# Feed-forward feature products: one instruction of 512 columns for both activation parts

## The reference, cut to what matters

```
def swiglu(x, w1, w3, w2):          # block 2, twice a layer
    return (silu(x @ w1) * (x @ w3)) @ w2
x = x + square(relu(h2 @ w_up)) @ w_down   # block 1, once a layer
```

## Time and profile before

| | us |
|---|---|
| median of 3 runs | 2420.14 (2417.0 to 2423.95) |
| the profiled execution | 2415.4 |
| its span | 2413.3 |
| TensorE busy | 2316.9 |
| VectorE busy | 1387.3 |
| ScalarE busy | 1118.4 |

### The profile page before, as it was taken

The page is one execution under the profiler, slowest core; times in us unless marked ns, Lnnn a source line. Parts: engine busy times, 40 slices in busy tenths (PEclk is TensorE's granted clock), DMA queues, the critical chain, the costliest instruction groups (busy, mean ns, idle before and its releaser), DMA issues.

```text
span 2413.3 us, 38462 instructions
## 1 busy us (share of the span) xinstructions
PE 2316.9 (96%) x16098; PEld 2123.8 (88%) x16098; DVE 1387.3 (57%) x1838; ACT 1118.4 (46%) x1737; POOL 186.8 (8%) x191
## 2 busy tenths in 40 slices
PE   7989999999999999999999999999999999998998
PEld 6988987887998998799998889979978999896997
DVE  5556555646654544655566764565565555776454
ACT  4754543573453444445443544444444444344442
POOL 0001210001120210000002001011100000110110
PEclk9999999999999999999999999999999999999999
DMA  6424555432555655564533545555555444263554
GB/s 215 136 97 148 181 198 172 167 123 100 180 187 188 220 184 189 163 181 140 168 109 119 174 164 182 187 201 184 187 167 184 154 157 141 79 205 125 187 180 141
DMA packets 109006, 395.93 MB, mean 164 GB/s; under 512 B 12375, under 2 KB 12545, under 8 KB 108577
## 3 DMA queue, kind: packets, MB, share of 16 engines
q1 hardware_dynamic: 104400, 377.53, 47.4%
q0 software_dynamic: 4432, 15.93, 2.0%
HBM read 392.92 MB, written 1.05 MB: 163 GB/s over the span
## 4 chain that ended last, share of the span: by engine, by line
PE 86%; DVE 7%; ACT 4%; DMA 2%; issue 1%; SPq 0%; DVEq 0%; ACTq 0%
PE psum L389 77%; DVE w_low L346 2%; PE psum L791 2%; PE psum L757 2%; DMA ring<-in_weights 2%; PE psum L693 2%; ACT w_high L343 1%; PE psum L775 1%; ACT attn_p L873 1%; DVE stats L563 1%; PE psum L1747 1%; DVE mx L817 0%; DVE xs L2059 0%; DVE xs L586 0%; DVE xT_low L652 0%
## 5 line engine op out<-in xcount | busy, mean ns | idle before, releaser
L346 DVE TENSOR_TENSOR w_low<-ring,w_high 128x1024 fp32r<-128x1024 f32 x704 | 863.0, 1255 | 588.3 <-ACT w_high L343 587.0
L343 ACT ACTIVATE w_high<-ring 128x1024 fp32r<-128x1024 f32 x704 | 717.5, 1053 | 295.0 <-DMA ring<-in_weights 294.9
L389 PE MATMUL psum<-xT_high,w_high 128*128 128x256 f32 x2976 | 848.7, 285 | 0.0
L389 PE MATMUL psum<-xT_low,w_high 128*128 128x256 f32 x2976 | 844.4, 284 | 0.0
L389 PE MATMUL psum<-xT_high,w_low 128*128 128x256 f32 x2976 | 844.3, 284 | 0.0
L389 PEld LDWEIGHTS psum<-xT_high,w_high 128*128 128x128 f32 x2976 | 573.0, 193 | 0.8
L389 PEld LDWEIGHTS psum<-xT_low,w_high 128*128 128x128 f32 x2976 | 573.1, 193 | 0.4
L389 PEld LDWEIGHTS psum<-xT_high,w_low 128*128 128x128 f32 x2976 | 573.0, 193 | 0.0
L389 PE MATMUL psum<-w_high,hidden 128*128 128x512 f32 x1216 | 377.0, 390 | 0.0
L389 PEld LDWEIGHTS psum<-w_high,hidden 128*128 128x128 f32 x1216 | 228.4, 188 | 47.0
L389 PE MATMUL psum<-w_low,hidden 128*128 128x512 f32 x608 | 236.8, 389 | 0.0
(11 more groups left out here) (233 smaller groups left out, 2201.9 us busy)
## 6 DMA issues: line engine op xcount, KB each, us to landing
ring<-in_weights SPq DMA_DIRECT2D x706, 512.0 KB, 3.6
pages<-in_affine POOLq DMA_DIRECT2D x16, 512.0 KB, 5.0
ring<-in_weights SPq DMA_DIRECT2D x8, 440.0 KB, 3.4
pages<-in_gains POOLq DMA_DIRECT2D x4, 512.0 KB, 5.1
pages<-in_mem POOLq DMA_DIRECT2D x2, 1024.0 KB, 6.2
ring<-in_weights SPq DMA_DIRECT2D x4, 384.0 KB, 3.2
x<-in_x_in SPq DMA_DIRECT2D x2, 512.0 KB, 4.5
pages<-in_rows POOLq DMA_DIRECT2D x2, 512.0 KB, 6.0
```

The source lines that it names most:

```text
L343: eng.activation(high, raw, ACT.Copy).then_inc(self.flag("w_rounded").sem, 1)
L346: eng.tensor_tensor(self.w_low[:, piece % SLOTS, 0:width], raw, high.bitcast(F32), ALU.subtract).then_inc(self.flag("w_split").sem, 1)
L389: m = pe.matmul(out, a, b, start=(first and i == 0), stop=(last and i == len(pairs) - 1))
```

## The change: what it does

`xT_high` and `xT_low` become the halves of one tensor `xT`. A new function `gemm_beside` gives each tile a bank of its own: per k a matmul of 256 columns (low weights by the high activation) into the bank's first half, and one of 512 columns (high weights by both activation parts, a moving operand of two runs of 256) into the whole bank. The first half then holds two of the three products and the second half the third. VectorE adds the halves with a `tensor_reduce` of 512 elements to 256 (`halves_added`). Block 1 takes 28 banks a layer for `up` in place of 14, block 2 takes 40 in a feed-forward part in place of 20. `gemm_features` stays for all other products.

In block 1 the maximum with zero moves from ScalarE to VectorE, in one instruction with the square. In block 2 silu reads the sum from SBUF. In both, the engines split weights after each tile, one piece a time.

```
-        self.xT_high = sb("xT_high", [P, KD, SEQ], F32R)
-        self.xT_low = sb("xT_low", [P, KD, SEQ], F32R)
+        self.xT = sb("xT", [P, 2, KD, SEQ], F32R)
+        self.xT_high, self.xT_low = self.xT[:, 0, :, :], self.xT[:, 1, :, :]
...
+    def gemm_beside(self, pe, l, stream, banks, group, act, kn, tile):
+        self.take_bank(pe, l, banks, group)
+        out = self.bank(banks, group)
+        for k in range(kn):
+            high, low = self.weight(pe, l, stream, (tile[0], tile[1], k))
+            act(k)
+            pe.matmul(out[:, 0:SEQ], low, self.xT_high[:, k, :], start=(k == 0), stop=False, skip_group_check=True)
+            m = pe.matmul(out.rearrange("p (x s) -> p x s", x=2), high, self.xT[:, :, k, :], start=False,
+                          stop=(k == kn - 1), skip_group_check=True)
+            if k == kn - 1:
+                m.then_inc(*self.flag("filled").one())
+            self.used(l, stream, (tile[0], tile[1], k), m, self.flag("filled").last(l) if k == kn - 1 else None)
+        self.piece_after[group] = self.piece_now
+
+    def halves_added(self, dve, l, banks, key, out):
+        h = self.filled(dve, l, banks, key)
+        dve.tensor_reduce(out, h.rearrange("p (x s) -> p s x", x=2), AX, ALU.add).then_inc(*self.drained(banks, key))
...
-                c.gemm_features(pe, l, stream, banks, "up", ("up", n), xTf, KD,
-                                [("up", 2 * n - 4), ("up", 2 * n - 3)])
+                for i in (2 * n, 2 * n + 1):
+                    c.gemm_beside(pe, l, stream, banks, ("up", i), xTf, KD, ("up", i - 4))
...
-                h = c.filled(act, l, banks, ("up", n))
-                act.wait_ge(*(c.flag("hidden_whole").at(l, n - 3) if n >= 4 else c.flag("first_whole").at(l, n - 1)))
-                act.activation(c.attn_p[:, n % 2, :], h, ACT.Relu).then_inc(*c.drained(banks, ("up", n)))
-                if n > 2:
-                    round_hidden(n - 1)
-                after(("up", n))
+                for i in (2 * n, 2 * n + 1):
+                    split(c.piece_after["up", i] + AHEAD)
+                    if i == 2 * n and n > 2:
+                        round_hidden(n - 1)
...
-                c.wait_drained(dve, l, banks, ("up", n))
-                if n >= 4:
-                    dve.wait_ge(*c.flag("hidden").at(l, n - 3))
-                dve.tensor_tensor(c.attn_pT[:, n % 2, :], c.attn_p[:, n % 2, :], c.attn_p[:, n % 2, :],
-                                  ALU.mult).then_inc(*c.flag("hidden_whole").one())
-                after(("up", n))
+                dve.wait_ge(*(c.flag("hidden").at(l, n - 3) if n >= 4 else c.flag("first_whole").at(l, n - 1)))
+                for i in (2 * n, 2 * n + 1):
+                    cut = slice(i % 2 * SEQ, (i % 2 + 1) * SEQ)
+                    c.halves_added(dve, l, banks, ("up", i), c.attn_p[:, n % 2, cut])
+                    c.wait_drained(dve, l, banks, ("up", i))
+                    sum_, whole = c.attn_p[:, n % 2, cut], c.attn_pT[:, n % 2, cut]
+                    dve.scalar_tensor_tensor(whole, sum_, 0.0, sum_, ALU.max, ALU.mult
+                                             ).then_inc(*c.flag("hidden_whole" if i % 2 else "dve_step").one())
+                    split(c.piece_after["up", i] + AHEAD)
...
-                    c.gemm_features(pe, l, stream, banks, f, (f, n), xT, KD, [(f + "a", n), (f + "b", n)])
+                    for x in "ab":
+                        c.gemm_beside(pe, l, stream, banks, (f + x, n), xT, KD, (f + x, n))
...
-                    if n >= 4:
-                        c.wait_drained(act, l, banks, (f + "t", n - 4) if n < 6 else (f, n - 4))
-                    act.activation(silu[:, n % 4, :], h[:, 0:SEQ], ACT.Silu).then_inc(*c.flag("silu").one())
...
+                    after_a = c.piece_after[f + "a", n] + AHEAD
+                    c.wait_drained(act, l, banks, (f + "a", n))
+                    act.activation(silu[:, n % 4, :], silu[:, n % 4, :], ACT.Silu).then_inc(*c.flag("silu").one())
                     if n > 2:
                         round_hidden(f, n - 1)
-                    after((f, n))
+                    split(after_a)
+                    after((f + "b", n))
...
-                    dve.tensor_tensor(gated[:, n % 4, :], silu[:, n % 4, :], c.bank(banks, key)[:, SEQ:2 * SEQ],
-                                      ALU.mult).then_inc(*c.drained(banks, key))
-                    after((f, n))
+                    elif n >= 4:
+                        c.wait_drained(dve, l, banks, (f + "t", n - 4))
+                    c.halves_added(dve, l, banks, (f + "a", n), silu[:, n % 4, :])
+                    after((f + "a", n))
+                    c.halves_added(dve, l, banks, (f + "b", n), gated[:, n % 4, :])
+                    dve.wait_ge(*c.flag("silu").at(l, done + n + 1))
+                    c.wait_drained(dve, l, banks, (f + "b", n))
+                    dve.tensor_tensor(gated[:, n % 4, :], silu[:, n % 4, :], gated[:, n % 4, :], ALU.mult
+                                      ).then_inc(*c.flag("gated").one())
+                    after((f + "b", n))
```

More of the change, by code:

```diff
@@ L990, in block_1 @@
             banks.add((key, n))
-    for key, n in (("out", 0), ("up", 16), ("down", 0)):
+    for key, n in (("out", 0), ("up", 32), ("down", 0)):
         for i in range(n):
-            banks.add(("upt", i) if i < 2 else (key, i))
+            if i not in (2, 3):
+                banks.add(("upt", i) if i < 2 else (key, i))
         if not n:
@@ L1520, in ffn_groups @@
         for n in range(KF2):
-            banks.add((f + "t", n) if n < 2 else (f, n))
+            if n < 2:
+                banks.add((f + "t", n))
+            else:
+                banks.add((f + "a", n))
+                banks.add((f + "b", n))
     def model_groups(key):
@@ L1831, in round_hidden @@
             def round_hidden(f, n):
-                c.wait_drained(act, l, banks, (f, n))
+                act.wait_ge(*c.flag("gated").at(l, (KF2 - 2 if f == "f2" else 0) + n - 1))
                 act.activation(c.hidden[KF2][0][:, n, :], gated[:, n % 4, :], ACT.Copy
@@ L1844, in ffn @@
                         beside()
-                    key = (f + "t", n) if n < 2 else (f, n)
-                    h = c.filled(act, l, banks, key)
-                    if n >= 4:
-                        c.wait_drained(act, l, banks, (f + "t", n - 4) if n < 6 else (f, n - 4))
-                    act.activation(silu[:, n % 4, :], h[:, 0:SEQ], ACT.Silu).then_inc(*c.flag("silu").one())
                     if n < 2:
+                        act.activation(silu[:, n % 4, :], c.filled(act, l, banks, (f + "t", n))[:, 0:SEQ], ACT.Silu
+                                       ).then_inc(*c.flag("silu").one())
                         if n == 1:
@@ L2038, in ffn @@
                         bias_low()
-                    dve.wait_ge(*c.flag("silu").at(l, done + n + 1))
-                    key = (f + "t", n) if n < 2 else (f, n)
+                    key = (f + "t", n)
                     if n < 2:
+                        dve.wait_ge(*c.flag("silu").at(l, done + n + 1))
                         dve.tensor_tensor(first[:, n, :], silu[:, n % 4, :], c.bank(banks, key)[:, SEQ:2 * SEQ], ALU.mult
@@ L2469 @@
                         "sb_valued", "osb_ready", "merged", "hidden_whole", "sink_less", "sink_exp"],
-           2: COMMON + ["params", "mem_loaded", "affine_in", "bias_cleared", "bias_rounded", "bias_parted", "pool_step", "silu", "bias_halved", "merged", "gmlp_normed",
+           2: COMMON + ["params", "mem_loaded", "affine_in", "bias_cleared", "bias_rounded", "bias_parted", "pool_step", "silu", "gated", "bias_halved", "merged", "gmlp_normed",
                         "spatial_ready", "spatially_mixed", "gmlp_gated", "convolved", "lat_ready", "n_roped",
@@ L2474 @@
 COUNTS = {
-    1: {'filled': 50,
-         'drained0': 13,
-         'drained1': 13,
-         'drained2': 12,
-         'drained3': 12,
-         'dve_step': 64,
+    1: {'filled': 64,
+         'drained0': 16,
+         'drained1': 16,
+         'drained2': 16,
+         'drained3': 16,
+         'dve_step': 78,
          'act_step': 16,
@@ L2512 @@
          'first_whole': 2},
-    2: {'filled': 123,
-         'drained0': 31,
-         'drained1': 31,
-         'drained2': 31,
-         'drained3': 30,
+    2: {'filled': 163,
+         'drained0': 41,
+         'drained1': 41,
+         'drained2': 41,
+         'drained3': 40,
          'dve_step': 165,
@@ L2555 @@
          'cmp_roped': 1,
-         'branch_gated': 2},
+         'branch_gated': 2,
+         'gated': 40},
 }
```

1 line of the change is left out of this document (added).

## The result

The changed kernel takes 2428.95 us (median of 8 runs, 2424.52 to 2433.23) against 2419.29 us for the kernel before in the same session (8 runs, 2415.73 to 2423.95): ratio 1.0039, 95% interval 1.0029 to 1.005. It is slower, by 9.7 us; the forecast was 2413.4 us. The value lies on the other side of no change. It is inside the range given (2398 to 2475) only because that range was drawn out to the dear reduce, which did not come true; the forecast's own range, 2403 to 2422, does not hold it.

The account below looks back on a forecast made before the run. TensorE was taken to bound the changed stages. From the profiled 2415.4 us, block 1 takes 6.0 and block 2 takes 0.7 (gain 17.1 against waits 16.4), giving 2408.7, or 2413.4 us on the median's scale; range 2398 to 2475.

Parts of the forecast that it names:

- the dear reduce: Rival: VectorE's reduce alternates between bank halves and takes 1.07 us, making block 2's loop 6.49 us; 2474 us, slower, chance 22%.
- the loop's sum of 5.73 us: Block 2: one VectorE and ScalarE round for two tiles takes 5.73 us against TensorE's 5.55, so VectorE falls behind 0.18 us.
- 0.02 (the product waits for it): Block 2's loop: the wait between the second reduce and VectorE's product, taken as 0.02 us on top of the reduce's 0.69.
- The pace of 0.3467 us a pair: TensorE, changed products: one 256-column and one 512-column matmul take 0.120 + 0.2267 = 0.3467 us, in place of 0.360.
- the gross gain: TensorE time saved by shorter products, before any waits: 23.0 us, of which 6.0 in block 1 and 17.1 in block 2.
- the third rival: The operand's second run costs another 13.3 ns, so a pair stays at 0.360 us; 2424.5 us, no change, chance 13%.
- -6.0 forecast: Block 1: VectorE needs 2.2 to 2.37 us a tile, under TensorE's 2.77, so the whole 6.0 us gain stays.
- L - 2.6 at the fourth bank: Block 2, start of each down product: TensorE waits VectorE's lateness L less 2.6 us; 2.2, 2.2, 4.2, 7.8, together 16.4 us.
- The limit beyond which products stop inside the stage: Block 2's feed-forward parts: VectorE's lateness over 7 us stalls products earlier, which costs the same microseconds.
- The cheap reduce: Rival: VectorE's reduce takes 0.42 us, block 2's loop is 5.19 us and hardly binds; 2398 us, faster, chance 10%.
- the forecast's own case: The main forecast without the rivals, chance 55%: range 2403 to 2422 us, split 0.23 faster, 0.30 within, 0.02 slower.
- three signs of being wrong: VectorE keeps level with TensorE in block 2, the reduce is away from 0.69 us by over 0.04, or block 1 shows waits.

Follow-up runs that it names:

- e1: Changed kernel, but in block 2 ScalarE rounds the weights five pieces ahead before waiting for the first reduce, not behind silu: 2399.85 us, ratio 0.9917 to the kernel before.
- e11: Changed kernel with VectorE's wait for silu moved ahead of the second reduce in block 2's loop: 2422.48 us, ratio 1.0017 to the kernel before.
- e4: Changed kernel with block 2 as in the kernel before, so only block 1 has the new form: 2415.39 us, ratio 0.9987 [0.9977, 0.9997].
- e9: Changed kernel with block 1 as in the kernel before, so only block 2 has the new form: 2435.14 us, ratio 1.0058 to the kernel before.
- e8: Changed kernel with one more VectorE instruction, a memset of 128 unused columns, in block 2's loop: 2434.8 us, ratio 1.0059 to the kernel before.

## Why the prediction failed

**The reason was right, one term of its sum was too small.** I said that VectorE falls behind in block 2 because of a loop through ScalarE's queue, that VectorE would idle 1.7 us there behind w_high, and that TensorE would pay at the start of each down product. All three are in the trace (1.74 us of idle; waits in all four parts), and e1 shows that the order makes them.

**The step that failed: the loop's sum of 5.73 us.** Its terms against the trace: reduce a to silu 0.72 (as taken), silu 0.32 (0.30), rounding 0.31 (0.30), w_high to w_low 1.08 (as taken), w_low 1.14 (as taken), reduce b to the product 0.79 (0.71), product 0.34 (as taken), w_low 1.14 (as taken). I counted "0.02 (the product waits for it)" where two waits stand in front of the product, which e11 prices at 0.07 us. At 68 us per microsecond the 0.10 us are 6.8 us of the 15.5 us by which I missed. It is the largest term and not the whole: with it alone put right, the forecast would have been 2420.2 us, no change; block 1, the pace and late weights, below, make the rest. The forecast's own range said "0.1 us of the loop's small gaps" moves it by 6 us; I kept the round's length at its middle all the same, where most unseen gaps can only add.

**The pace of 0.3467 us a pair** held in some stages only, and in none for the first 48 pairs. In block 1, where nothing else binds, a slow stage gives 1.2 us less. In block 2 it matters less than it seems, since a faster product would have waited longer: at the slow pace the gross gain is 8.5 us in place of 17.1, and lateness grows by 5.83 - 5.65 = 0.18 us with every n, by chance what I had. The bound above that I set for it, the third rival (no gain at all, 0.360 us), was too far; nothing I had read showed the middle.

**Block 1: -6.0 forecast, -3.7 measured alone** (between -0.7 and -5.6 by e4's interval). VectorE keeps up there, as forecast: no wait of TensorE in the product stages. The pace explains some 0.6 us of the difference in every trace (the first 48 pairs of two stages) and 1.2 more where a stage is slow; the rest is within the interval.

**Lateness and waits.** "L - 2.6 at the fourth bank": the second parts paid 2.4 and 2.2 us where I had 2.2 each. The first parts paid 6.6 and 7.8 us where I had 4.2 and 7.8; of the missing 2.4 in the first one, 2.1 come from its first round, n = 2, where ScalarE waited 1.10 and 2.08 us for weights that had not landed and the round took 7.6 us (808.24 to 815.85) in place of the 5.53 us of the other parts. That, too, comes and goes: the same round took 5.45 us in e11. I had read such a wait at the start of the other first part only. The limit beyond which products stop inside the stage is 7 us as worked out (4.4 us of waits at the down product and 2.6), but it was reached after some six of the eighteen rounds in one first part and four in the other. And the wait is not only at the fourth bank: the weights of the down product and the second bank are late too.

The sum, an estimate: 6.8 us from the loop, 2.3 from block 1, 2.1 from the late weights in one part (as in the profiled execution), 1.4 from the slow pace in block 2 (at a loop of 5.73 us block 2 would then have lost 0.7 us instead of gaining 0.7). Some 3 us are left, of the size of what the clock and late transfers change between executions; their cause was not shown.

**The rivals.** The dear reduce (1.07 us, 22%) is out: 686 ns with the two values of each sum 1 KB apart in a bank, where the reduction of as many elements to 2 outputs takes 683. I had said of the rule on PSUM lines in the Trainium skill, "Advanced Engine Details and Errata", section "Memory Cachelines", that by it this rival would be likelier; for VectorE's reading of PSUM in this form the runs don't bear it out. The cheap reduce is out by the same number. The outcome on the slower side came by a mechanism I had forecast and not by the one I had given the chance to: the chance for slower inside the forecast's own case was 0.02, though the loop's 0.1 us was known to decide it. None of my three signs of being wrong came true either: they asked whether VectorE is late, what a reduce takes and whether block 1 waits, and none asked for the length of the round, which failed.

## What to carry to other kernels

When a change moves work from one engine to another, write down the ring of waits it makes (who waits in its queue behind whom) and its round time; if that lies within a few per cent of what the bound engine needs (here 5.83 against 5.65 us), each 0.1 us of a gap is paid once a round, and a forecast of a small gain is not safe until the ring is cut. Here the cut was one line: what another engine will need (rounding the next weights) goes ahead of a wait, not behind it, and it turned +0.4% into -0.8%. Where an instruction needs two semaphores and sits on such a ring, put the wait that is satisfied early in front of an earlier instruction.

## What was new about the hardware

- A second wait in front of one VectorE instruction costs 0.07 us though its semaphore was set long before (0.79 against 0.72 us from reduce to product; ratio to before 1.0039 against 1.0017).
- Matmuls of 256 and 512 columns in turn run at 0.3467 or 0.3533 us a pair at the same granted clock of 1.00; the pace changes where TensorE is held, if only for some 2 ns, and is not tied to the layout of the operand. Two and two, they ran at 0.3483 us a pair in 12 stages of 12.
- After waits of about 2 us the granted clock of TensorE can be 0.52 for some 3.5 us, a loss of some 1.7 us (behind two of four down products in e9, four of four in e8), and at other times, after the same waits, stay at 1.00 (the changed kernel's profiled execution).
